# Two retention pieces per head freed from the gate buffer, one piece moved, and new planner constants, in a two-layer hybrid trunk

## The chip, the core and the metric

The kernel runs on one core of one Trainium2 chip (trn2). A core has five engines that run side by side, each through its own instructions in order: TensorE (PE, matrix multiplication and transposes), VectorE (DVE), ScalarE (ACT), GpSimd (POOL) and SyncE (SP, which here only issues DMAs). They meet through semaphores. The metric is the device time of one execution in microseconds; the number given for a kernel is the median of its runs.

## The reference

Two layers are computed over 1024 rows of width 1024. Each layer normalizes its input, multiplies it by one wide matrix (`w_in`), feeds the columns to three groups of heads, joins their outputs, multiplies by `w_out`, normalizes and adds to the input. Cut to what matters:

```
h = rmsnorm(x, pre_norm)
proj = einsum('bld,de->ble', h, w_in)
(gq, gk, gv, gz, gb, ga, sx, sB, sC, sz, sdt, rq, rk, rv, rg) = split_cols(proj, IN_SIZES)
qkv = silu(causal_conv(concat([gq, gk, gv]), gdn_conv))            # gated DeltaNet, 4 heads of 128
o_a = rmsnorm(gated_deltanet(...), gdn_norm) * silu(gz)
xbc = silu(causal_conv(concat([sx, sB, sC]), ssd_conv) + ssd_conv_b) # state space, 16 heads of 64, 2 groups
o_b = rmsnorm(ssd(...) * silu(sz), ssd_norm)
q_c, k_c = rotary(rq), rotary(rk)                                  # retention, 4 heads of 128
o_c = rmsnorm(retention(q_c, k_c, rv), ret_norm) * silu(rg)
x = x + rmsnorm(concat([o_a, o_b, o_c]) @ w_out, post_norm)
```

The DeltaNet solves, for each head and each chunk, a unit lower triangular system. Everything is float32; the kernel keeps that accuracy by splitting each factor of the large products into a high and a low part and summing three products.

## The kernel before

**Parts and pieces.** The work is cut into four parts, p = 0 to 3: two halves of 512 rows in each of two layers. Within a part, `w_in` is taken in 26 pieces of 256 columns, in the order of the list `PIECES` (L50): gate pieces of the DeltaNet ("gz"), its q, k, v ("gdn"), the B and C of the state space ("bc"), its gates ("sz", group, half) and inputs ("sx", group, half), and last eight retention pieces ("ret", 0) to ("ret", 7). The even retention pieces hold query and key of a head, the odd ones its value and gate. A piece has two halves, each with its own PSUM bank out of two, and a half is made in eight slices; a slice is 6 matmuls of 256 columns or 3 of 512.

**Weights.** Pieces go through a ring of two buffers (`W_RING`). A piece is loaded when the piece two before it has been used. ACT rounds it into the high part (L2147, four steps), and POOL subtracts to get the low part (L2433, four steps). Parts 0 and 2 do this for all pieces; they store the low parts in DRAM (the "keep" DMA, L1305), and parts 1 and 3 load them from there (L1302) beside the raw weights, so POOL has nothing to do. The pieces numbered in `AGAIN` (L63) are excepted: they are split again in parts 1 and 3 and not kept.

**Mixers.** Between the slices PE does the small products of the mixers. For the triangular systems a block of size `BASES[p]` (L39) on the diagonal is inverted on DVE column by column (`gdn_base`, L1844 to L1870), and then the inverse is doubled level by level on PE and DVE (`gdn_p`, `gdn_xx`; L1889, L1899, L1902) until it has 128 rows. `BASES` is (8, 16, 16, 16): part 0 has four levels, the others three. The finished rows of a group of heads stand in one of two gate buffers; `mix_turn` transposes them, and the units of the output projection (`out`, 24 matmuls each) use them.

**Gate buffers.** `gate_of` gives the gate buffer of a piece and `frees` (L877) lists the steps that must stand earlier in the order than a piece. A gate piece may come only after the `mix_turn` that read the buffer's earlier contents; so ("sz", 1, *) needs the `mix_turn` of DeltaNet heads (head 3 for the last piece), and every retention piece needs `mix_turn` of state-space group 0 (p, 1). A retention piece also needs its slot, which `x_turn` of the state space gives free.

**The order.** It is not made on the chip. `make_plan` (L242) keeps a clock for each engine with fixed costs, and puts out one list of steps; each engine runs its share of that list in that order. When several steps could be next, constants decide (L786 to L797). `OUT_WAIT` is the wait of the next mixer step above which an output unit is put in, provided that `APART` slices have passed since the last one; `LATE` says when a slice counts as late, so that an output unit goes first; `KEEP` and `HOLD` hold the last units of the second-last output group back.

Of the kernel before, what the change touches and what calls it, by code (L numbers as in the profile page):

```python
# [35 lines left out]
NDEC = GH + SH  # L36
NSM = GH + NDEC
LEVELS = 7
BASES = (8, 16, 16, 16)  # L39
FIRSTS = [n.bit_length() - 1 for n in BASES]  # L40
SIZES = sorted(set(BASES))
LOWEST, WIDEST = min(FIRSTS), max(BASES)
COPIES = 8
# [3 lines left out]

PC = 256
N_GDN_PC, N_GZ, N_BC, N_SZ, N_SX, N_RET = 6, 2, 2, 2, 2, 8
PIECES = ([("gz", 0), ("gdn", 0), ("gdn", 1), ("gz", 1), ("bc", 0), ("gdn", 2), ("gdn", 3), ("bc", 1),  # L50
           ("sz", 0, 0), ("gdn", 4), ("sz", 0, 1), ("gdn", 5), ("sz", 1, 0), ("sx", 0, 0), ("sx", 0, 1), ("sx", 1, 0),
           ("sx", 1, 1), ("sz", 1, 1)]
          + [("ret", i) for i in range(N_RET)])
AT = {piece: i for i, piece in enumerate(PIECES)}


def m_of(piece, half):

    return {"gdn": 0, "bc": 12}.get(piece[0], 16 + 4 * piece[1]) + 2 * piece[-1] + half


NTH = {m: n for n, m in enumerate(m_of(piece, half) for piece in PIECES if piece[0] in ("gdn", "bc", "sx") for half in range(2))}
AGAIN = range(3)  # L63
W_RING = 2
Q = KD
SBUF = 224 * 1024 - 1
# [65 lines left out]
def base_parts(size):  # L132

    out = [("mask", ()), ("sum", ())]
    for i in range(0, size, COPIES):
        out += [("copy", range(j, min(j + 4, i + COPIES))) for j in range(i, i + COPIES, 4)]
        out += [("column", range(j, min(j + 2, i + COPIES, size - 1))) for j in range(i, min(i + COPIES, size - 1), 2)]
    return out + [("spread", ()), ("turn", ())]


BASE_PARTS = [base_parts(n) for n in BASES]
BASE_END = [len(parts) - 1 for parts in BASE_PARTS]
# [50 lines left out]
def front_steps():  # L193
# [3 lines left out]
    def add(step, *needs):  # L197
        out.append((step, needs))
# [9 lines left out]
    for p in range(PARTS):  # L208
        for i, piece in enumerate(PIECES):
            for half in range(2):  # L210
                last = p + 1 < PARTS and (i, half) == (len(PIECES) - 1, 1)
                needs = list(frees(p, i, half))
                if i == 0 and p >= 2:
                    needs.append(("final", p - 2, NT - 1))
                if last:
                    for t in range(2):
                        add(("norm", p + 1, t), ("rescale", p + 1, t), *needs)
                if i == len(PIECES) - 2 and p + 1 < PARTS:
                    add(("scale", p + 1, half), ("ssd_y", p, SG - 1, NT - 1), *([("final", p - 1, NT - 1)] if p else []))
                for q in range(Q):  # L220
                    j, odd = divmod(Q * half + q - SPLIT_FROM, 2)
                    if 0 <= j < 4 and not odd and len(PIECES) * p + i + 1 < PARTS * len(PIECES):
                        add(("split", *((p, i + 1) if i + 1 < len(PIECES) else (p + 1, 0)), j))
# [18 lines left out]
def make_plan():  # L242
# [120 lines left out]
    def play(step):  # L363
# [9 lines left out]
        def mark(name, time):  # L373
            at[name] = time
# [99 lines left out]
        elif k == "gdn_base":  # L474
# [5 lines left out]
            elif part == "copy":  # L480
                mark("n", dve(len(cols) * (230 + 2 * BASES[p]), *after))
            elif part == "column":
                mark("n", dve(len(cols) * 2 * (220 + 2 * BASES[p]), *after))
            else:
# [231 lines left out]
    def due(step):  # L716
        return max([at.get(e, 0) for e in needs(step)] + [bank_due(step)])

    mix_at = inv_at = pre_at = front_at = apart = 0
    while mix_at < len(mix) or inv_at < len(inv) or pre_at < len(pre) or front_at < len(front) or outs or turns or any(sides.values()):  # L720
# [26 lines left out]
        if front_at < len(front) and front[front_at][0][0] == "split_small" and not ring_free():  # L747
            front_needs.append(("ring", ))
        wait = due(step) - now if step else OUT_WAIT + 1
        late = not front_needs and due(front[front_at][0]) > now + LATE  # L750
        stuck = any(n and n[0] not in ("split", "rescale") for n in front_needs) or front_at == len(front)
        unit = outs[0] if outs and ("small", smalls) in done and (outs[0][2] or not outs[0][1] or ("final", outs[0][1] - 1, NT - 1) in done) and (outs[0][1] % 2 or ("split_out", *outs[0][1:4]) in done) else None
        if unit and unit[1:3] == (PARTS - 1, GROUPS - 2):
            if front_at < len(front) and not stuck and len(outs) <= KEEP or front_at == len(front) and step and wait < HOLD:
                unit = None
        if unit and due(unit) <= now + NEAR and (late or stuck or wait > OUT_WAIT and apart >= APART):
            emit(outs.pop(0))
# [28 lines left out]
GATE_WAIT = 0  # L786
TABLE_WAIT = 1500
NORM_WAIT = 3000
OUT_WAIT = 1000000000.0
LATE = 200  # L790
SPLIT_FROM = 6
APART = 16
KEEP = 6
RELOAD = 4400
HOLD = 250
NEAR = 0
AHEAD = 2000  # L797
FAR = 1e12
# [16 lines left out]
def is_split(n):  # L815

    p, i = divmod(n, len(PIECES))
    return p % 2 == 0 or i in AGAIN


def is_kept(n):

    p, i = divmod(n, len(PIECES))
    return p % 2 == 0 and i not in AGAIN

# [45 lines left out]
def gate_of(p, i):  # L871

    kind = PIECES[i][0]
    return {"gz": 4 * p, "sz": 4 * p + 1 + (PIECES[i][1] if kind == "sz" else 0), "ret": 4 * p + 3}.get(kind)


def frees(p, i, half):  # L877
    need = []
    n = slot_of(p, i, half)
    if slot_owner(n) is not None:  # L880
        need.append(slot_reader(slot_owner(n)))
    g = gate_of(p, i)
    if g is not None and g >= 2:
        need.append(("mix_turn", p, 0, 2 * PIECES[i][2] + 1) if g % 4 == 2 else ("mix_turn", (g - 2) // 4, (g - 2) % 4))
    if PIECES[i] == ("sx", 0, N_SX - 1) and half == 1:
        need += [("gdn_p", p, GH - 2, LEVELS - 1, j) for j in range(2)]
    if PIECES[i] == ("sx", SG - 1, N_SX - 1) and half == 1:
        need += [("gdn_xx", p, GH - 1, LEVELS - 1, j) for j in range(2)]
    if PIECES[i][0] == "bc" and p:
        need.append(("ssd_y", p - 1, SG - 1, NT - 1))  # L890
    return need
# [52 lines left out]
def hybrid_kernel(nc, x, w_in, w_small, w_out, cons, rope, pars, rows, post_norm, out):  # L944
# [15 lines left out]
    with ExitStack() as ctx:  # L960
# [1129 lines left out]
        def _(act):  # L2090
# [20 lines left out]
            for s in plan:  # L2111
# [77 lines left out]
                elif k == "proj" and s[4] == Q - 1:  # L2189
# [33 lines left out]
                    elif kind in ("gz", "sz"):  # L2223
                        j = PIECES[i][-1]
                        G = gate_of(p, i)
                        gate_wait(act, G, p, PIECES[i])
                        empty(A(gate[:, G % 2, 2 * half:2 * half + 2, j * PC:(j + 1) * PC],
                                bank(tag).rearrange("p (t n) -> p t n", t=2), ACT.Silu), tag)
                    elif PIECES[i][1] % 2:
                        h = PIECES[i][1] // 2  # L2230
                        G = gate_of(p, i)
                        gate_wait(act, G, p, PIECES[i])
                        b = bank(tag).rearrange("p (t n) -> p t n", t=2)
                        v = slot_at(10 * p + 6 + h)[:, 1024:1536].rearrange("p (t n) -> p t n", t=NT)
                        slot_wait(act, 10 * p + 6 + h)
                        A(v[:, 2 * half:2 * half + 2, :], b[:, :, 0:P], ACT.Copy)
                        empty(A(gate[:, G % 2, 2 * half:2 * half + 2, h * P:(h + 1) * P], b[:, :, P:2 * P], ACT.Silu), tag)
# [248 lines left out]
```

How the kernel before makes its waits and increments, by code:

```python
        def wait_filled(eng, tag):  # L1097
            eng.wait_ge(filled[bank_of[tag]], use_of[tag] + 1)
# [1 line left out]
        def wait_emptied(eng, tag):  # L1100
            eng.wait_ge(emptied[bank_of[tag]], use_of[tag] + 1)
# [94 lines left out]
        def slot_wait(eng, n):  # L1196
            if slot_owner(n) is None:
                return
            r = slot_reader(slot_owner(n))
            if r[0] == "gdn_open":
                wait_filled(eng, (*r, "a"))
                eng.wait_ge(S["gdn_kq"], GH * r[1] + r[2] + 1)
            elif r[0] == "x_turn":
                wait_filled(eng, (*r, NT - 1))
            else:
                wait_filled(eng, r)
# [22 lines left out]
        @block.sync  # L1230
# [3 lines left out]
                if kind == "later":  # L1234
                    sp.dma_start(con[:, C_LEV:], cons[:, C_LEV:]).then_inc(later, 16)
                    for l in range(1, DEPTH):
                        sp.dma_start(par[:, l, :], pars[l]).then_inc(later, 16)
                elif kind == "x":
                    if n >= NT:
                        wait_filled(sp, ("norm", (n - 2) // NT, (n - 2) % NT, 1))
                    if p and key[2] < 2:
                        wait_filled(sp, ("ssd_y", p - 1, SG - 1, NT - 1, "w"))
                    if p >= 2:
                        sp.wait_ge(x_stored[key[2]], 16 * (p - 1))
                    sp.dma_start(x_tile(n), x_rows(p, key[2])).then_inc(x_in[n if n < 4 else n % 2], 16)
                elif kind == "rest" and p == PARTS - 1:
                    wait_filled(sp, ("ret_o", p, RH - 1, NT - 1))
```

## Time and profile before

| | |
|---|---|
| median of 3 runs | 2102.42 us (2098.83 to 2102.58) |
| the profiled execution, its own time | 2098.74 us |
| its span, from the first to the last instruction | 2096.9 us |
| PE busy | 2042.2 us |
| DVE busy | 1414.8 us |
| ACT busy | 995.7 us |
| POOL busy | 516.1 us |

The span is what the instructions of the core take; the execution's own time is 1.8 us more. An engine's busy time counts matmuls that overlap in the pipeline once. Parts are not marked in the profile. By the order of the matmuls, the slices of part 0 run from 14 to 494 us, of part 1 to 1001 us, of part 2 to 1529 us and of part 3 to 2028 us; after that come the last output units, to 2085 us. The granted clock of TensorE is given as a share of full speed: 1.0 is 2.4 GHz and 0.5 is 1.2 GHz.

### The profile page before, as it was taken

The page shows a single profiled execution, that of the slowest core. Times are in us where ns is not written, and L with a number is a line of the kernel's source. Part 1 is how long each engine was busy: PE and PEld are TensorE (multiplying, and loading weights), DVE is VectorE, ACT ScalarE, POOL GpSimd, SP SyncE. Part 2 cuts the span into 40 slices and gives each one's busy share as a digit, 9 for nine tenths or more (in the row PEclk, how much of TensorE's full clock was granted, in tenths as well). Part 3 has the DMA queues.
Part 4 walks back from the last instruction along what each step waited for, and adds up shares of the span by engine and source line. Part 5 has one row for each costly group of instructions (what it writes and reads, how often), then busy time and mean ns, then how long its engine had stood idle before and what let it go on. Part 6 is the DMA issues. An engine that isn't in the chain of part 4 may idle for free.

```text
span 2096.9 us, 38540 instructions
## 1 busy us (share of the span) xinstructions
PE 2042.2 (97%) x14692; PEld 1885.2 (90%) x14692; DVE 1414.8 (67%) x3324; ACT 995.7 (47%) x1985; POOL 516.1 (25%) x456
## 2 busy tenths in 40 slices
PE   7999999999999999999999999899999999999997
PEld 6888888999989988999889897899989899899997
DVE  5788767546668877734578888675566788766334
ACT  5644376434554447633454344664345444574211
POOL 3443343432101102201243334334320011121001
PEclk9999999999999999999999999999999999999999
DMA  4543255545555635344354436455546546453434
GB/s 167 169 141 99 106 185 174 191 153 191 196 176 181 212 131 208 134 160 135 120 189 141 141 113 210 161 182 171 190 131 233 180 162 212 150 181 121 161 108 185
DMA packets 88119, 343.57 MB, mean 164 GB/s; under 512 B 10048, under 2 KB 11136, under 8 KB 81536
## 3 DMA queue, kind: packets, MB, share of 16 engines
q1 hardware_dynamic: 87360, 340.69, 47.8%
q8 instruction: 118, 1.93, 0.4%
q14 instruction: 65, 0.53, 0.1%
q10 hardware_dynamic: 576, 0.41, 0.1%
HBM read 250.72 MB, written 90.34 MB: 163 GB/s over the span
## 4 chain that ended last, share of the span: by engine, by line
PE 87%; DVE 5%; issue 4%; ACT 3%; POOL 1%; DMA 0%; POOLq 0%; DVEq 0%; SPq 0%; ACTq 0%
PE ps L1367 83%; PE ps L1370 4%; POOL w_low L2433 1%; ACT wk L2306 0%; ACT w_hi L2147 0%; POOL rs L2390 0%; ACT L2242 0%; DVE base L1862 0%; DVE wo_parts L1990 0%; DVE base L1863 0%; DMA wk<-in_x 0%; DVE wk L1934 0%; DVE slot L1759 0%; ACT raw L2207 0%; ACT slot L2242 0%
## 5 line engine op out<-in xcount | busy, mean ns | idle before, releaser
L1367 PE MATMUL ps<-w_hi,hT_hi 128*128 128x256 f32 x1792 | 524.5, 293 | 4.7 <-POOL w_low L2433 3.0
L1367 PE MATMUL ps<-w_hi,hT_lo 128*128 128x256 f32 x1792 | 504.0, 281 | 0.0
L1367 PE MATMUL ps<-w_low,hT_hi 128*128 128x256 f32 x1792 | 502.7, 281 | 0.0
L2433 POOL TENSOR_TENSOR w_low<-w_loaded,w_hi 128x512 fp32r<-128x512 f32 x232 | 314.1, 1372 | 470.9 <-ACT w_hi L2147 470.7
L1367 PEld LDWEIGHTS ps<-w_hi,hT_hi 128*128 128x128 f32 x1792 | 340.3, 190 | 11.8 <-POOL w_low L2433 4.3
L1367 PEld LDWEIGHTS ps<-w_low,hT_hi 128*128 128x128 f32 x1792 | 338.1, 189 | 5.0 <-issue 4.3
L1367 PEld LDWEIGHTS ps<-w_hi,hT_lo 128*128 128x128 f32 x1792 | 338.2, 189 | 0.0
L1367 PE MATMUL ps<-hT_hi,w_hi 128*128 128x512 f32 x768 | 319.0, 415 | 5.2 <-POOL w_low L2433 5.2
L1367 PE MATMUL ps<-hT_hi,w_low 128*128 128x512 f32 x768 | 304.0, 396 | 0.0
L1367 PE MATMUL ps<-hT_lo,w_hi 128*128 128x512 f32 x768 | 303.6, 395 | 0.0
L1367 PE MATMUL ps<-wo_parts,mixT_hi 128*128 128x256 f32 x960 | 269.9, 281 | 0.0
L1759 DVE SCALAR_TENSOR_TENSOR slot<-raw,par,slot 128x512 f32<-128x512 f32 x222 | 190.6, 859 | 17.3 <-ACT slot L2220 11.5
L2004 DVE TENSOR_TENSOR acc<-acc,ps 128x512 f32<-128x512 f32 x96 | 65.6, 686 | 184.4 <-PE ps L1367 177.4
L1367 PEld LDWEIGHTS ps<-wo_parts,mixT_hi 128*128 128x128 f32 x960 | 180.9, 188 | 3.3 <-issue 2.4
L1367 PEld LDWEIGHTS ps<-hT_hi,w_hi 128*128 128x128 f32 x768 | 145.5, 189 | 32.8 <-POOL w_low L2433 7.0
L1367 PEld LDWEIGHTS ps<-hT_lo,w_hi 128*128 128x128 f32 x768 | 144.6, 188 | 32.7
L1367 PEld LDWEIGHTS ps<-hT_hi,w_low 128*128 128x128 f32 x768 | 145.4, 189 | 24.9 <-issue 0.2
L2147 ACT ACTIVATE w_hi<-w_loaded 128x512 fp32r<-128x512 f32 x232 | 135.2, 623 | 64.6 <-DMA w_loaded<-in_w_in 64.5
L1367 PE MATMUL ps<-wk 128*128 128x128 f32 (+2 forms) x1008 | 156.5, 287 | 2.4 <-issue 1.3
L1367 PEld LDWEIGHTS ps<-wk 128*128 128x128 f32 x1008 | 135.0, 192 | 21.3 <-issue 10.4
L2147 ACT ACTIVATE w_hi<-w_raw 128x512 fp32r<-128x512 f32 x184 | 107.8, 622 | 81.3 <-DMA w_low<-w_low_kept 81.2
L1367 PE MATMUL ps<-wo_hi,mixT_hi 128*128 128x256 f32 x480 | 139.6, 291 | 4.3 <-DVE wk L2008 2.9
(225 smaller groups left out, 3969.3 us busy)
## 6 DMA issues: line engine op xcount, KB each, us to landing
w_loaded<-in_w_in SPq DMA_DIRECT2D x116, 512.0 KB, 5.1
w_low_kept<-w_low SPq DMA_DIRECT2D x46, 1024.0 KB, 8.1
w_raw<-in_w_in SPq DMA_DIRECT2D x92, 512.0 KB, 5.8
w_low<-w_low_kept SPq DMA_DIRECT2D x92, 512.0 KB, 6.7
wo_loaded<-in_w_out SPq DMA_DIRECT2D x32, 512.0 KB, 4.1
wk<-cum_rows SPq DMA_DIRECT2D x32, 512.0 KB, 3.8
wo_split<-wo_parts SPq DMA_DIRECT2D x32, 512.0 KB, 7.7
wo_parts<-wo_split SPq DMA_DIRECT2D x28, 512.0 KB, 4.4
```

Of the source, the lines that this page charges most:

```text
L1367: return nc.tensor.matmul(o, a, b, start=start, stop=stop)
L1370: return nc.tensor.transpose(o, a, ident)
L1759: stt(o, r[:, j:j + HALF], w[:, j:j + 1], o, ALU.mult, ALU.add).then_inc(S["conv_done"], 1)
L2004: empty(tt(o, o, b, ALU.add), s)
L2147: A(high, source, ACT.Copy).then_inc(S["w_hi_ready"], 1)
L2433: tt(w_lo[at], wr[at], w_hi[at], ALU.subtract)\
```

## The change

Six things differ, and everything else follows from the list of steps that the planner makes of them:

- `gate_of` gives no gate buffer for even retention pieces (query and key). They have no gate columns, and `frees` therefore no longer asks for `mix_turn` (p, 1) before them.
- ("ret", 0) stands ahead of ("sz", 1, 1) in `PIECES`. Among the DeltaNet and B/C pieces the order becomes gdn 2, bc 0, bc 1, gdn 3 (it was bc 0, gdn 2, gdn 3, bc 1).
- `BASES[2]` is 8, so part 2 inverts blocks of 8 and doubles over four levels, as part 0 does.
- `AGAIN` is pieces 1 and 2; piece 0, ("gz", 0), is kept in DRAM by parts 0 and 2 and loaded by parts 1 and 3.
- `OUT_WAIT` is 1000, `LATE` 0, `KEEP` 2 and `HOLD` 0.
- The plan follows from all these.

```
-BASES = (8, 16, 16, 16)
+BASES = (8, 16, 8, 16)
...
-PIECES = ([("gz", 0), ("gdn", 0), ("gdn", 1), ("gz", 1), ("bc", 0), ("gdn", 2), ("gdn", 3), ("bc", 1),
+PIECES = ([("gz", 0), ("gdn", 0), ("gdn", 1), ("gz", 1), ("gdn", 2), ("bc", 0), ("bc", 1), ("gdn", 3),
            ("sz", 0, 0), ("gdn", 4), ("sz", 0, 1), ("gdn", 5), ("sz", 1, 0), ("sx", 0, 0), ("sx", 0, 1), ("sx", 1, 0),
-           ("sx", 1, 1), ("sz", 1, 1)]
-          + [("ret", i) for i in range(N_RET)])
+           ("sx", 1, 1), ("ret", 0), ("sz", 1, 1), ("ret", 1), ("ret", 2), ("ret", 3), ("ret", 4), ("ret", 5),
+           ("ret", 6), ("ret", 7)])
...
-AGAIN = range(3)
+AGAIN = range(1, 3)
...
-OUT_WAIT = 1000000000.0
-LATE = 200
+OUT_WAIT = 1000
+LATE = 0
...
-KEEP = 6
+KEEP = 2
...
-HOLD = 250
+HOLD = 0
...
-    return {"gz": 4 * p, "sz": 4 * p + 1 + (PIECES[i][1] if kind == "sz" else 0), "ret": 4 * p + 3}.get(kind)
+    return {"gz": 4 * p, "sz": 4 * p + 1 + (PIECES[i][1] if kind == "sz" else 0), "ret": 4 * p + 3 if PIECES[i][1] % 2 else None}.get(kind)
```

## Rows read from the trace of the kernel before

**Rows 1.** Page: busy time, share of the span, number of instructions; TensorE.

```profile
PE 2042.2 (97%) x14692; PEld 1885.2 (90%) x14692; DVE 1414.8 (67%) x3324; ACT 995.7 (47%) x1985; POOL 516.1 (25%) x456
```

**Rows 2.** Windows: stretch, length, busy us of each engine (instructions), clock, DMA.

```profile
600.00:800.00 200.00, 200.00 (x1323) 180.85 (x1322) 155.80 (x465) 99.17 (x192) 20.50 (x24) 1.00 0.52 174
1200.00:1300.00 100.00, 95.14 (x621) 85.57 (x620) 84.95 (x206) 43.25 (x90) 40.40 (x34) 0.98 0.46 156
1300.00:1345.00 45.00, 39.02 (x249) 34.23 (x247) 31.52 (x47) 26.69 (x60) 16.79 (x13) 0.92 0.38 129
```

**Rows 3.** Waits of PE, 1100 to 1345 us: total us, times, longest.

```profile
PE ps L1370 <- DVE gate L1955: 5.5, 1, 5.5
PE ps L1367 <- POOL w_low L2433: 4.3, 2, 3.1
PE ps L1367 <- DVE st_g L1927: 1.9, 1, 1.9
```

**Rows 4.** Waits of PE, 300 to 345 us.

```profile
PE ps L1367 <- DVE wk L1692: 1.5, 1, 1.5
PE ps L1367 <- DVE wk L2008: 1.4, 1, 1.4
```

**Rows 5.** Windows at half clock, columns as in rows 2.

```profile
323.60:327.00 3.40, 3.40 (x12) 2.37 (x11) 3.40 (x7) 0.00 (x0) 0.00 (x0) 0.50 0.68 231
1197.40:1200.80 3.40, 3.40 (x11) 2.69 (x9) 2.08 (x19) 0.76 (x2) 0.29 (x1) 0.50 0.94 337
1289.60:1293.00 3.40, 3.40 (x14) 3.12 (x13) 3.33 (x6) 0.78 (x2) 1.29 (x1) 0.50 0.40 166
1323.70:1330.50 6.80, 3.47 (x16) 3.47 (x17) 4.22 (x5) 6.77 (x18) 4.18 (x4) 0.50 0.06 22
```

**Rows 6.** Timeline of PE, 1310 to 1330 us: start, us, instruction, idle before it.

```profile
1319.65 1.91 PE L1370 MATMUL ps<-con,slot 128*128 128x128 f32 x16
1327.03 1.11 PE L1370 MATMUL ps<-con,gate 128*128 128x128 f32 x4 [5.47 <-DVE gate L1955]
```

**Rows 7.** Chain that ended last, 895 us on: start, us, matmuls.

```profile
895.74 31.86 PE ps L1367 x272
```

**Rows 8.** Windows, DVE with tile base, in parts 0, 1 and 2.

```profile
60.00:280.00 220.00, 32.93 (x132) 0.99 0.40 133
500.00:820.00 320.00, 41.08 (x260) 1.00 0.52 173
1000.00:1310.00 310.00, 58.13 (x260) 0.99 0.45 151
```

**Rows 9.** Lines by form, DVE, 60 to 280 us: count, busy us, mean ns.

```profile
L1902 DVE TENSOR_TENSOR slot<-ps,con 128x256 f32<-128x256 f32 x32 | 12.6, 402 | 2.6 <-PE ps L1367 2.5
L1889 DVE TENSOR_TENSOR wk<-wk,ps 128x256 f32<-128x256 f32 x24 | 9.5, 414 | 2.2 <-PE ps L1367 1.8 <-DVE wk L1908 0.2
L1899 DVE STREAM_TRANSPOSE wk<-wk 128x256 f32<-128x256 f32 x16 | 6.9, 431 | 0.0
```

**Rows 10.** Timeline of PE, 110 to 131 us: the products of one step, then a slice.

```profile
123.44 1.05 PE L1367 MATMUL ps<-slot,wk 128*128 128x128 f32 x8
124.25 0.48 PE L1367 MATMUL ps<-hT_hi,w_hi 128*128 128x512 f32 x1
```

**Rows 11.** DMA issues: count, KB each, median us to landing.

```profile
w_loaded<-in_w_in SPq DMA_DIRECT2D x116, 512.0 KB, 5.1
w_low_kept<-w_low SPq DMA_DIRECT2D x46, 1024.0 KB, 8.1
w_low<-w_low_kept SPq DMA_DIRECT2D x92, 512.0 KB, 6.7
```

**Rows 12.** Timeline of SP's queue, 0 to 110 us: the load of piece 2.

```profile
29.47 0.81 SPq L1299 DMA_DIRECT2D w_loaded<-in_w_in  x2
```

**Rows 13.** Waits of all engines, whole span, columns as in rows 3.

```profile
DVE et L2036 <- POOL et L2411: 19.7, 4, 7.3
```

**Rows 14.** Lines by form, DVE, 345 to 495 us: emptying a retention piece's bank.

```profile
L1784 DVE TENSOR_TENSOR slot<-ps,rp 128x256 f32<-128x256 f32 x16 | 6.7, 417 | 3.9 <-PE ps L1367 3.3 <-DVE gate L1969 0.6
```

## The prediction

> **What bounds the kernel now.** I read the engines' busy times first. PE is busy for 2042.2 us of the span, and no other engine reaches 70% [rows 1]. The reader should see that little can be won: a kernel bound by one engine can lose only that engine's idle time, its time at half clock, or work. So I looked for these stretch by stretch. In the DeltaNet stretch of part 1 PE is never idle in 200 us, although DVE is busy for 78% of it [rows 2]. Part 2 is different. In the 100 us from 1200 us on PE is idle for 4.9 us with DVE at 85%, and in the 45 us after that for 6.0 us with the clock at 0.92 [rows 2]. The waits of PE name the reasons: one of 5.5 us for the last step of a DeltaNet head (L1955), two of 4.3 us in all for low weights, and 1.9 us behind DVE [rows 3]. A second, smaller place is the first state-space group of part 0 [rows 4]. Four stretches at half clock lie beside these places: 3.4 us at 323.6, 1197.4 and 1289.6 us, and 6.8 us at 1323.7 us [rows 5]. Waits of the other engines count only where PE shows them.
>
> **The retention piece as filler.** In part 2 PE ends the 16 transposes of `x_turn` at 1321.6 us and stands until 1327.0 us, for `mix_turn` of head 3 [rows 6]. The order had nothing else to give it: ("sz", 1, 1) needs that very `mix_turn`, part 1's output units were used up, and the retention pieces stood behind. After the change ("ret", 0) needs only `x_turn` and stands next. 272 narrow matmuls take 31.86 us, 117 ns each, so a half of 48 takes 5.6 us and the piece 11.2 us [rows 7]. That is more than the wait of 5.5 us. The wait goes, and the half clock at 1323.7 us with it: for 3.3 of its 6.8 us PE stood anyway; in the other 3.5 us it worked at half rate and lost 3.5 / 2 = 1.75 us [rows 5, 6]. Gain: 5.5 + 1.75 = 7.2 us. The lower end is nothing, if the planner still puts `mix_turn` straight behind `x_turn`.
> In part 0 the same piece can stand among the steps of state-space group 0, where PE waits 1.5 + 1.4 us and then works 3.4 us at half clock, a loss of 1.7 us [rows 4, 5]. Together that is 4.6 us. These waits stand at single steps behind DVE's masks, and a filler helps only where the order puts it into the right gap. Between 0 and 4.6 us I take two thirds, 3.0 us, since the order is made from clocks that know of masks. What is moved is no new work: the loads follow the use of the ring, and the matmuls are the same. Parts 1 and 3 still have output units as filler in this stretch, so they gain nothing.
>
> **Blocks of 8 in part 2.** Removed on DVE: the base steps cost 58.1 us in part 2, and with blocks of 8 in part 0, also beside POOL's subtractions, 32.9 us; 25.2 us less [rows 8]. Added on DVE: one level for 4 heads, each with two masks (402 ns), two subtractions (414 ns) and two transposes (431 ns): 4 x 2 x 1.247 = 10.0 us [rows 9]. DVE is relieved by 15.2 us. Added on PE: 4 heads x 2 halves x (4 + 4) = 64 matmul instructions. Eight of them take 0.81 us from their start to that of the next slice, so 64 take 6.5 us [rows 10].
> The Trainium skill (TensorE: Matmul & The Clock Gate, section Back-to-back issue gap) gives about 81 ns per matmul of 128 columns in a stream with its weight loads. As an estimate the 64 would cost 5.2 us by it; the row has 101 ns for each, and the measurement decides.
> What DVE's relief gives to PE is bounded by what PE loses there beside the 5.5 us: 1.9 us behind DVE and 4.3 us behind the split of weights [rows 3], and two half clocks of 3.4 us, 1.7 us each [rows 5]: 9.6 us. The lower end is 0. The wait behind DVE and the half clocks should go (1.9 + 3.4 us). Of the 4.3 us I take 3.5: POOL's subtraction is slow beside DVE's many small steps, but it also hangs on the load before it. That is 8.8 us; net of the matmuls, 8.8 - 6.5 = 2.3 us gained.
> The same 260 base steps take 58.1 us in part 2 and 41.1 us in part 1, where POOL hardly subtracts [rows 8]. The Trainium skill (SBUF — State Buffer, section Who interferes with whom) says that a DVE step with two SBUF inputs and a GpSimd step hold a shared port in turn, and the loser waits for the whole instruction. By that rule the added steps, which read PSUM or one SBUF input, keep their price whatever POOL does. It would leave the 10.0 us as they are.
>
> **Piece 0 kept.** Parts 1 and 3 save four subtractions and load 1 MB more; parts 0 and 2 store 1 MB more. In parts 1 and 3 a load is issued two pieces ahead, so it has one piece of 11.2 us before its first slice [rows 7], and one of these lands in 6.7 us [rows 11]. In part 0 the store stands on SP's queue ahead of the load of piece 2, which needs its buffer: today that load is issued at 29.5 us [rows 12]. The store can begin when the four low parts are made, about 28 us by the order of POOL's steps, lands after 8.1 us, and the load after another 5.1 us [rows 11], at 41 us; ACT and POOL then need 2 us, and piece 2 starts at 45 us. This is close. I take 0, with 3 us of loss and 1 us of gain as bounds. Behind the store on SP's queue stand the loads of piece 2 and of the next output unit, which ACT splits; no mixer step waits for them yet.
>
> **Order of the DeltaNet pieces and the constants.** Head 1 gets its keys one piece (11 us) earlier, head 2 one piece later; head 2 opens only after head 1 in both orders. `OUT_WAIT` and `LATE` let output units in sooner, so that fewer are left later, above all at the end of part 3, where nine stand behind its last slice. Bounds: 4 us either way, a bit less than two such waits as the longest here [rows 3]; 0 taken. For waits at new places in a new order I add 2.0 us, one wait like the 1.9 us of today [rows 3].
>
> **Sum.** -7.2 - 3.0 - 2.3 + 2.0 = -10.5 us. Against the profiled execution, 2098.7 us, that gives 2088.2 us. The median of the runs before stands 3.7 us above that execution, so the forecast for a median is 2091.9, say 2092 us.
>
> **Rivals.** (a) *All of it works.* The 4.6 us of part 0 and the 9.6 us of part 2 go in full, and no new wait comes: -7.2 - 4.6 - 9.6 + 6.5 = -14.9 us, 2087.5 us; with the constants' 4 us it ends at 2083.5, and with what I can't see in rows somewhat below. For it: the part 1 stretch shows PE without idle time beside a DVE nearly as busy [rows 2].
> (b) *The wait moves.* The planner's clock thinks head 3 done earlier than it is and puts its `mix_turn` ahead of the retention piece or after a slice or two of it. Then the 7.2 us stay, and 3.0 + 2.3 - 2.0 = 3.3 us are left: 2099 us; with the lower ends of the other terms more than 2102. For it: the order before was made by the same clock and was wrong by 5.5 us there [rows 3]. Against: DVE, whose lateness makes it wrong, is relieved by 15.2 us. That the change doesn't do what it says (the piece comes no earlier, since its slot needs `x_turn` anyway) gives the same time.
> (c) *The retention piece stalls its own bank: slower.* The piece in this place, ("sz", 1, 1), is emptied by ACT in one step. ("ret", 0) is emptied by DVE, in order, in four steps of 0.42 us [rows 14], and DVE stands in waits of its own in the state-space stretch: up to 7.3 us for POOL (L2036) [rows 13]. A bank has 5.6 us of cover, the other half [rows 7]. With 1.7 us for emptying, the deciding point is a DVE wait of 3.9 us. The longest row would cost 7.3 + 1.7 - 5.6 = 3.4 us. If four of the eight halves met such a wait, 13.6 us, and two of these brought a half clock of 1.7 us, it would be -10.5 + 17.0 = +6.5 us, 2109 us. Against: the four such waits sum to 19.7 us, a mean of 4.9 us, just over the point [rows 13].
>
> **Chances.** Forecast (2087 to 2097) 0.48; (a), below that, 0.17; (b) 0.20, of which 0.04 below 2098.2; (c) 0.15. About 0.2%, 4.2 us, is what a measurement of this kernel can tell from no change. Faster 0.48 + 0.17 + 0.04 = 0.69; same 0.16 of (b) and 0.01 of (c), 0.17; slower 0.14. The range leaves out the outer half of (c) and the far end of (a): 2080 to 2109 us.
>
> **What would show it.** In the changed kernel's trace the wait for L1955 behind `x_turn` of part 2 is gone, and matmuls of a narrow piece stand there; the half clock at about 1324 us is gone; DVE's base steps in part 2 take about 33 us in 132 instructions; PE has 14692 + 64 matmuls; its idle time between 1200 and 1345 us falls from 10.9 us to under 4. If PE waits for DVE's L1786, which empties the bank, (c) is at work; if it waits for L2147 or L2433 near 45 us or at the start of part 1 or 3, the kept piece is. Wrong at the root would be a large gain or loss in parts 1 and 3 or at the end: then the constants decide, which I put at 0.

## The result, and the profile after

The changed kernel takes 2105.75 us (median; 2101.69 to 2108.64), the kernel before 2101.08 us beside it (2098.83 to 2103.48). The ratio is 1.0021, 95% interval 1.0013 to 1.0030: it is slower by about 4.7 us, where I had forecast 2092 us. The profiled span is 2102.9 us, 6.0 us longer than before. (The title counts wrongly: of the two retention pieces of each head one is freed, the one with query and key.)

The page of the changed kernel, and windows of part 2 (stretch, length, busy us of PE, PEld, DVE, ACT, POOL with instructions, clock, DMA). They answer to [rows 1] and [rows 2]:

```profile
PE 2052.4 (98%) x14756; PEld 1894.6 (90%) x14756; DVE 1417.3 (67%) x3220; ACT 1002.9 (48%) x1991; POOL 514.8 (24%) x448
...
1200.00:1300.00 100.00, 98.13 (x650) 87.74 (x649) 73.36 (x150) 41.05 (x88) 39.60 (x36) 1.00 0.54 186
1300.00:1345.00 45.00, 43.16 (x296) 37.92 (x295) 31.05 (x55) 29.31 (x61) 19.16 (x14) 1.00 0.41 141
```

DVE alone with tile base, in the stretch of part 2, answers to the last of [rows 8]:

```profile
1000.00:1310.00 310.00, 32.80 (x132) 1.00 0.47 157
```

In part 2 the signs that I had named came true. Idle time of PE between 1200 and 1345 us fell from 10.9 to 3.7 us, the clock of that stretch is 1.00, the base steps take 32.8 us. The waits of PE from 1100 to 1345 us (total, times, longest) no longer hold the 5.5 us for L1955, and those for L2433 fell from 4.3 to 1.3 us [rows 3]:

```profile
PE ps L1367 <- POOL w_low L2433: 1.3, 3, 0.8
PE ps L1367 <- DVE slot L1902: 0.9, 3, 0.5
```

So the time was lost elsewhere. The waits of PE over the whole span show two groups that before did not have at all, L2147 and the DMA of `wo_parts`:

```profile
PE ps L1370 <- ACT wk L2123: 9.1, 1, 9.1
PE ps L1367 <- POOL w_low L2433: 8.8, 9, 2.5
PE ps L1367 <- ACT w_hi L2147: 4.2, 2, 2.2
PE ps L1367 <- DMA wo_parts<-wo_split: 2.9, 1, 2.9
```

The 9.1 us are in both kernels. The half clock stretches have moved: in place of those at 323.6, 1197.4, 1289.6 and 1323.7 us [rows 5] there are these (besides one near 61 us and one behind the last matmuls, which both kernels have):

```profile
294.90:301.70 6.80, 6.10 (x27) 5.81 (x28) 3.59 (x3) 6.74 (x13) 2.29 (x2) 0.50 0.45 186
516.70:520.10 3.40, 3.40 (x18) 3.40 (x18) 0.69 (x1) 3.40 (x5) 0.74 (x2) 0.50 0.16 58
2059.60:2063.00 3.40, 3.40 (x18) 3.40 (x17) 0.00 (x0) 0.00 (x0) 0.00 (x0) 0.51 1.03 417
```

**An account of the whole span.** A window that is 5 us worse says little when the order of steps differs. So I gave each matmul its step of the planned order, took the time from the start of each step to that of the next, and took as usual length of a kind of step the 15th percentile of the kernel before. What a step has above it is a stall where it is 0.25 us or more, and small excess where it is less. This holds both waits and half clock. It is my own working from the starts of the matmuls, in us:

| kernel | first to last matmul | usual work | small excess | stalls | part 0 | part 1 | part 2 | part 3 | end |
|---|---|---|---|---|---|---|---|---|---|
| before | 2072.8 | 1942.5 | 64.9 | 65.4 | 22.0 | 5.6 | 28.4 | 5.6 | 0.5 |
| after | 2078.8 | 1948.4 | 68.2 | 62.2 | 25.4 | 9.2 | 11.2 | 7.9 | 5.2 |

(Another 3.3 us of stalls lie before the first slice, in all kernels. The account is of one execution. A second profiled execution of experiments 1, 2 and 3 differs in single columns by up to 2 us, so smaller differences between kernels say nothing.) Part 2 has 17.2 us less of stalls. Against it stand 5.9 us of matmuls of the added level, 3.3 us of small excess, and stalls: 3.4 us in part 0, 3.6 us in part 1, 2.3 us in part 3, 4.7 us at the end. The sum is +6.0 us.

### The profile page after: what moved, and what is told of

Read it like the earlier page. It is cut to its first block, busy times and chain, and to the rows that moved or that the text cites. A ratio compares the mean times of both kernels' runs of the same rounds, so it can differ in the third digit from the quotient of the medians.

```text
span 2102.9 us, 38565 instructions
## 1 busy us (share of the span) xinstructions
PE 2052.4 (98%) x14756; PEld 1894.6 (90%) x14756; DVE 1417.3 (67%) x3220; ACT 1002.9 (48%) x1991; POOL 514.8 (24%) x448
## 4 chain that ended last, share of the span: by engine, by line
PE 82%; DVE 5%; issue 4%; DMA 4%; ACT 3%; POOL 1%; SPq 1%; POOLq 0%; DVEq 0%; ACTq 0%
PE ps L1367 79%; PE ps L1370 4%; DMA wo_split<-wo_parts 1%; DMA w_low_kept<-w_low 1%; DMA wk<-in_x 1%; DVE slot L1759 1%; POOL w_low L2433 1%; ACT wk L2306 0%; DMA wk<-x_mid 0%; ACT w_hi L2147 0%; DVE hT_lo L1711 0%; ACT L2242 0%; DVE acc L2082 0%; ACT wk L2297 0%; DVE wo_parts L1990 0%
## 5 line engine op out<-in xcount | busy, mean ns | idle before, releaser
L2433 POOL TENSOR_TENSOR w_low<-w_loaded,w_hi 128x512 fp32r<-128x512 f32 x224 | 310.4, 1403 | 436.8 <-ACT w_hi L2147 436.8
L2147 ACT ACTIVATE w_hi<-w_raw 128x512 fp32r<-128x512 f32 x192 | 112.2, 623 | 104.7 <-DMA w_low<-w_low_kept 104.7
L1367 PEld LDWEIGHTS ps<-wk 128*128 128x128 f32 x1024 | 135.6, 191 | 21.0 <-issue 11.5
L2147 ACT ACTIVATE w_hi<-w_loaded 128x512 fp32r<-128x512 f32 x224 | 129.7, 621 | 39.4 <-DMA w_loaded<-in_w_in 39.4
```

The source lines that it names most:

```text
L1367: return nc.tensor.matmul(o, a, b, start=start, stop=stop)
L2147: A(high, source, ACT.Copy).then_inc(S["w_hi_ready"], 1)
L2433: tt(w_lo[at], wr[at], w_hi[at], ALU.subtract)\
```

## The experiments

All ratios are to the kernel before on the same chip, with the 95% interval; one part in a thousand is 2.1 us. A difference of two ratios is uncertain by 1.2 to 2.0 in a thousand, by their intervals. The stalls named in this section are from the account above.

**1. The retention part alone**, in the kernel before.

```
-           ("sx", 1, 1), ("sz", 1, 1)]
-          + [("ret", i) for i in range(N_RET)])
+           ("sx", 1, 1), ("ret", 0), ("sz", 1, 1)]
+          + [("ret", i) for i in range(1, N_RET)])
...
-    return {..., "ret": 4 * p + 3}.get(kind)
+    return {..., "ret": 4 * p + 3 if PIECES[i][1] % 2 else None}.get(kind)
```

> The kernel before with the gate freed for even retention pieces and (ret, 0) ahead of (sz, 1, 1), and nothing else; the planner makes the order again. Theory A (this part of the change is worth what was forecast, and the loss comes from other parts): PE's 5.5 us wait for L1955 in part 2 and the half clock beside it go, 7 us; part 0 gives back 3 us, since the weights of (ret, 0) come late there; 2097 us against 2101 before, ratio 0.998. Theory B (the freed piece only moves the waits, here too): 2101 us or more, ratio 1.000 or above.

Measured: 1.0044 [1.0030, 1.0058], 9 us slower. The wait for L1955 in part 2 is gone, and stalls there fell from 28.4 to 22.3 us; but part 0 has 31.4 in place of 22.0 us, and the end 3.8 in place of 0.5. The waits of PE from 340 to 372 us are new:

```profile
PE ps L1367 <- ACT wk L2297: 4.0, 1, 4.0
PE ps L1370 <- ACT gate L2324: 4.0, 1, 4.0
```

L2324 makes the gated rows that `mix_turn` (0, 1) transposes, and ("ret", 1) still needs that `mix_turn`, since odd pieces keep their gate columns. The piece that used to stand between had been used 11 us earlier, and few output units were left as cover. The wait had moved by one piece: from `mix_turn` of head 3 to `mix_turn` of state-space group 0.

**2. Blocks of 8 in part 2 alone**, in the kernel before.

```
-BASES = (8, 16, 16, 16)
+BASES = (8, 16, 8, 16)
```

> The kernel before with blocks of 8 in part 2 and nothing else. Theory A (the level pays for itself): the 64 added matmul instructions cost 6 us, the waits behind DVE and the half clocks between 1100 and 1303 us give 8 us; 2099 us, ratio 0.999. Theory B (DVE's relief is not what PE lacked, the matmuls are simply added): 2106 us, ratio 1.002 to 1.003; then this alone would be the whole loss of the changed kernel.

Measured: 1.0003 [0.9995, 1.0012]. PE is busy for 2048.7 us, 6.5 us more; DVE for 1400.8 us, 14.0 us less; part 2 has 21.4 us of stalls in place of 28.4 (20.7 us in a second execution). The matmuls of the added level take what the relief of DVE gives. In this order PE still waits for L1955, by the same 5.5 us:

```profile
PE ps L1370 <- DVE gate L1955: 5.5, 1, 5.5
```

**3. Piece 0 split again**, in the changed kernel.

```
-AGAIN = range(1, 3)
+AGAIN = range(3)
```

> The changed kernel with piece 0 split again in parts 1 and 3, as before (AGAIN = range(3)); the rest of the order stays almost the same. Theory A (the kept piece costs the two waits for L2147 at the third slice of part 1 and of part 3): both waits of 2.2 us and the half clock near 517 us go; 2100 us against 2105.7 for the changed kernel, ratio to before 0.9995. Theory B (the waits there come from the later output units and the order, not from the load): the waits stay, 2105 us, ratio 1.002.

Measured: 0.9993 [0.9985, 1.0002]. The loss is gone: 2.8 in a thousand less than the changed kernel, 5.9 us. Stalls of part 1 and 3 are 5.4 and 6.0 us, as before. But it isn't the 10 us gain that I forecast either.

**4. The old `OUT_WAIT`** in the changed kernel.

```
-OUT_WAIT = 1000
+OUT_WAIT = 1000000000.0
```

> The changed kernel with OUT_WAIT at 1e9 again, the rest as changed. Theory A (the earlier output units cost the end of part 3, where PE waits 2.9 us for the weights of a unit and then runs at half clock, and 3 us of switching between slices and units): 2099 us, ratio to before 0.999. Theory B (the constant is neutral, the loss at the end comes from somewhere else): 2105 us, ratio 1.002.

Measured: 1.0048 [1.0034, 1.0062]. The constant is worth 2.7 in a thousand, 5.7 us, in the new order. (Both theories expected it to cost or to do nothing.) Putting back `KEEP` and `HOLD` leaves the list of steps as it is, word for word; they do nothing here.

**5 and 6. The order apart from the data path.** The planner reads `AGAIN` too, so experiment 3 also changed the order. Here the plan is made with one value and the kernel built with the other.

```
+    global AGAIN
+    own, AGAIN = AGAIN, PLAN_AGAIN
     plan = make_plan()
+    AGAIN = own
```

Experiment 5 has `AGAIN = range(3)` and `PLAN_AGAIN = range(1, 3)`: the changed kernel's order, with piece 0 split again. Experiment 6 has them the other way round: the order of experiment 3, with piece 0 kept.

> The changed kernel's order of steps to the last one (its planner still believes that piece 0 is kept), but piece 0 is in fact split again in parts 1 and 3 and not stored. Theory A (the data path: 1 MB more to load and to store delays the loads of x, behind which ACT's fourth split of piece 0 stands): the waits of PE at the third and fourth slice of parts 1 and 3 go, ratio to before 0.9993 as with AGAIN = range(3), 2099 us. Theory B (the planner's order, with the split of an output unit put later, makes those waits): ratio 1.002, 2105 us, with the waits in place.

> The mirror image: the order of the kernel with AGAIN = range(3), but piece 0 is kept and loaded. Theory A (data path): PE waits for L2147 come back at the start of parts 1 and 3, ratio 1.002, 2104 us. Theory B (order): none, ratio 0.9993, 2099 us. Together with the run before this splits the 6 us between the two; if both land midway, both matter.

Measured: experiment 5 0.9992 [0.9983, 1.0000], experiment 6 1.0001 [0.9992, 1.0009]. The order of the changed kernel alone is not at fault. Keeping the piece costs 2.9 in a thousand in it (6.1 us); in the order of experiment 3 it costs 0.8 (1.7 us), which is within the uncertainty. How the loss comes about is seen at the start of part 1. First the longest wait of SP's queue from 489 to 505 us, then SP, ACT and PE from 488 to 516 us, all of the changed kernel (start, us, instruction, idle before it):

```profile
SPq L1331 <- DMA wo_split<-wo_parts: 10.4, 1, 10.4
```

```profile
488.38 0.33 SPq L1301 DMA_DIRECT2D w_raw<-in_w_in  x1
488.75 0.43 SPq L1302 DMA_DIRECT2D w_low<-w_low_kept  x1
...
491.01 0.53 SPq L1310 DMA_DIRECT2D wo_split<-wo_parts  x1
501.96 0.33 SPq L1335 DMA_DIRECT2D wo_loaded<-in_w_out  x1
...
503.28 1.41 SPq L1305 DMA_DIRECT2D w_low_kept<-w_low  x1
504.73 2.61 SPq L1245 DMA_DIRECT2D wk<-in_x  x2
```

```profile
513.33 1.06 ACT L2119 ACTIVATE junk<-wk 128x1024 f32<-128x1024 f32 x1 [5.21 <-DMA wk<-in_x]
...
514.38 0.61 ACT L2147 ACTIVATE w_hi<-w_raw 128x512 fp32r<-128x512 f32 x1
```

```profile
515.04 0.38 PE L1367 MATMUL ps<-w_hi,hT_hi 128*128 128x256 f32 x1 [2.19 <-ACT w_hi L2147]
```

Read it from the end, that is from the wait of PE. PE waits 2.19 us for the fourth rounding step of ("gz", 0). ACT takes its steps in order, and that one stands behind the norm of the next rows of x (L2119), which waits 5.21 us for its load. The weights had landed, since three of the four steps were done. The load of x is issued at 504.73 us without a wait of its own, straight behind what stands ahead of it on SP's queue, and that queue had stood 10.4 us, until 501.96, for the store of an output unit's low part (L1310, 491.01) to land. That store was issued right behind the kept piece's loads, which bring 1 MB more. In experiment 5, with the same order and no kept piece, SP and ACT have these lines (its line numbers are four higher):

```profile
SPq L1335 <- DMA wo_split<-wo_parts: 7.1, 1, 7.1
```

```profile
502.96 1.57 SPq L1249 DMA_DIRECT2D wk<-in_x  x2
...
509.13 1.06 ACT L2123 ACTIVATE junk<-wk 128x1024 f32<-128x1024 f32 x1 [3.74 <-DMA wk<-in_x]
...
510.18 0.62 ACT L2151 ACTIVATE w_hi<-w_loaded 128x512 fp32r<-128x512 f32 x1
```

The same store lands 3.3 us sooner after its issue, the load of x lands 6.2 us after its issue in place of 8.6, ACT's fourth step begins 4.2 us earlier, and PE does not wait. In the changed kernel the half clock at 516.7 us follows the wait. Part 3 begins with the same wait, of 2.0 us.

In experiment 6 the piece is kept too, and ACT's fourth step is nearly as late, at 513.4 us. But its order has 24 matmuls of an output unit (from 512.92 us) and `ret_s` between the third slice and the fourth, which begins only here:

```profile
516.56 0.37 PE L1371 MATMUL ps<-w_hi,hT_hi 128*128 128x256 f32 x1
```

In the changed kernel the same 24 matmuls stand behind the fourth slice. So at this place the loss needs two things together: the kept piece makes the load of x late, and the order made for it has moved the filler away.

**7. Keeping the piece alone**, in the kernel before.

```
-AGAIN = range(3)
+AGAIN = range(1, 3)
```

> The kernel before with one edit: piece 0 is kept in DRAM and loaded in parts 1 and 3 instead of split again; order and constants stay those of before. Theory A (keeping costs by itself, because its loads and stores crowd SP's queue at the starts of parts, whatever the order): slower by about 6 us, ratio 1.002 to 1.004, with PE waits for L2147 at the starts of parts 1 and 3. Theory B (keeping costs only together with the order of the changed kernel, in which the loads of part 0's output units and of x stand late): no wait for L2147 there, ratio 0.999 to 1.001.

Measured: 1.0032 [1.0019, 1.0045], 6.7 us slower. The size is that of theory A, but the wait isn't where either theory had it: PE never waits for L2147. Lines of SP, ACT and PE from 480 to 499 us, for piece 0 kept:

```profile
480.52 1.21 SPq L1245 DMA_DIRECT2D wk<-in_x  x2
...
488.75 1.06 ACT L2119 ACTIVATE junk<-wk 128x1024 f32<-128x1024 f32 x1 [5.53 <-DMA wk<-in_x]
...
492.95 0.59 ACT L2330 ACTIVATE wk<-ps 128x512 f32<-128x512 f32 x1
...
493.60 0.65 PE L1370 MATMUL ps<-con,gate 128*128 128x128 f32 x4 [1.56 <-ACT wk L2330]
...
498.96 0.68 PE L1367 MATMUL ps<-slot,wk 128*128 128x128 f32 x4 [1.69 <-issue]
```

and of the kernel before:

```profile
478.20 1.20 SPq L1245 DMA_DIRECT2D wk<-in_x  x2
...
485.00 1.06 ACT L2119 ACTIVATE junk<-wk 128x1024 f32<-128x1024 f32 x1 [5.36 <-DMA wk<-in_x]
...
488.67 0.60 ACT L2330 ACTIVATE wk<-ps 128x512 f32<-128x512 f32 x1
```

x is issued 2.3 us later, because the planner, which takes the kept piece into its clocks, puts an output unit ahead of PE's step that frees the buffer; and it lands 8.2 us after its issue in place of 6.8. So it arrives 3.75 us later, and L2330, behind L2119 on ACT, is 4.3 us late. Here the step that PE misses is not the split of the piece but L2330, a step of retention's last head. This comes twice, before part 1 and before part 3, with 1.6 + 1.7 and 1.4 + 1.7 us of waits, 6.4 us. The profiled execution is 9.2 us longer than that of the kernel before; much of the rest is in part 2, where the half clock near 1290 us is 6.8 us long in place of 3.4. (For the 1.7 us the profile names no releaser; that they come from the same delay is inferred.)

**8. The old order of the DeltaNet and B/C pieces**, with piece 0 split again.

```
-AGAIN = range(1, 3)
+AGAIN = range(3)
...
-PIECES = ([("gz", 0), ("gdn", 0), ("gdn", 1), ("gz", 1), ("gdn", 2), ("bc", 0), ("bc", 1), ("gdn", 3),
+PIECES = ([("gz", 0), ("gdn", 0), ("gdn", 1), ("gz", 1), ("bc", 0), ("gdn", 2), ("gdn", 3), ("bc", 1),
```

> The changed kernel with piece 0 split again, and the DeltaNet and B/C pieces in their old order (bc 0, gdn 2, gdn 3, bc 1). It is to be read against the same kernel with the new order (0.9993 of before). Theory A (the order of these pieces is worth nothing, as forecast): 0.998 to 1.001. Theory B (it is part of why stalls in part 2 fell): above 1.002, with the lost time in part 2 before 1320 us.

Measured: 1.0038 [1.0025, 1.0050] against 0.9993 with the new order. The order that I priced at nothing is worth 4.5 in a thousand, 9.4 us. Theory B has the size, but not the place: part 2 has 10.7 us of stalls with the old order and 12.4 with the new. The time is lost in part 0 (26.6 against 24.8), part 1 (9.2 against 5.4), part 3 (11.5 against 6.0) and at the end (5.4 against 3.3). In part 0 PE waits, from 340 to 372 us:

```profile
PE ps L1370 <- ACT gate L2324: 5.5, 1, 5.5
```

In the new order head 3 ends later: its `mix_turn` stands at 300 us, not at 285 us. The output units that need it start at 308 us in place of 295 us, and four of them stand between `x_turn` (0, 1) and `mix_turn` (0, 1), not two. At 2.8 us each they cover the 5.5 us. So the later head keeps the fillers back for the place where they are needed. The other parts, 1 and 3, were not followed to single waits.

**9. The retention part with the new `OUT_WAIT`**, in the kernel before: experiment 1 and

```
-OUT_WAIT = 1000000000.0
+OUT_WAIT = 1000
```

> The kernel before with the retention part (even pieces need no gate buffer, ret 0 ahead of sz 1 1) and OUT_WAIT 1000; LATE, KEEP, HOLD, bases, piece order and piece 0 as before. The retention part alone was 1.0044 of before. Theory A (the loss came from output units used up early, so that nothing covered the wait for ret 1's gate in part 0; OUT_WAIT changes when they are used): the 8 ms-style stall at 349 to 369 us of part 0 shrinks from about 12 us to under 4 us and the ratio is 0.998 to 1.001. Theory B (the loss is the retention part's own, whatever the constant): ratio 1.003 to 1.006.

Measured: 1.0064 [1.0050, 1.0078]. Both theories miss, B by little. I had thought that the constant was the partner that makes the retention part pay. It isn't: stalls of 3.8 + 5.8 + 1.3 us stand again around `mix_turn` (0, 1), and with the old piece order the constant costs 2.0 in a thousand, as much as the uncertainty of this difference, where it earns 2.7 with the new.

**10. The changed kernel without the retention part**, with piece 0 split again: the edit of experiment 1 undone.

> The changed kernel with AGAIN = range(3) and with the retention part of the change taken back: the gate buffer is waited for by all eight pieces, and (ret, 0) stands behind (sz, 1, 1). Theory A (freeing the retention pieces only moves the waits, as in the first experiment, where it cost 9 us alone): the wait for L1955 in part 2 is back, but part 0 and the end give as much or more; ratio 0.997 to 0.999, at or below AGAIN = range(3). Theory B (with output units let in early, OUT_WAIT = 1000, the freed piece is worth its 5 us and more): ratio 1.001 to 1.003.

Measured: 1.0029 [1.0018, 1.0040] against 0.9993 with it. In the new order the retention part earns 3.6 in a thousand, 7.6 us. Without it the waits of PE from 1300 to 1400 us are

```profile
PE ps L1370 <- DVE gate L1955: 5.5, 1, 5.5
PE ps L1370 <- ACT gate L2324: 2.7, 1, 2.7
```

so the wait of [rows 6] is back with its old length, with blocks of 8 too. Two more things stand in its account (in the table of the next section). Part 0 has 23.4 us of stalls, against 24.8 with the retention part and 22.0 in the kernel before: PE waits 2.8 us for L1955 where the changed kernel waits for its weights. And the end has 0.5 us of stalls in place of 3.3, with no wait for `wo_parts`. That wait is there in every kernel with the retention part and the old place of the loads of x, from 2.6 to 3.9 us, and in none without the part.

**11. The last loads of x behind those of the tail**, with piece 0 split again. At the end of part 3 the changed kernel issues four loads of x between the loads of the output units. The key by which a load is put into SP's queue is raised:

```
-            loads.append((where["ret_o", p, RH - 1, NT - 1] if p == PARTS - 1 else
+            loads.append((max(where["ret_o", p, RH - 1, NT - 1], where["out", PARTS - 1, GROUPS - 2, UNITS - 3, NT // 2 - 1]) + 0.5 if p == PARTS - 1 else
```

> The changed kernel with AGAIN = range(3), and at the end of part 3 the four loads of x for the last step stand on SP's queue behind the loads of the last output units, not ahead of them. Theory A (these 2 MB stand ahead of the load for unit (3, 2, 3), for which PE waits 2.6 us and then works at half clock): the wait for wo_parts at about 2050 us goes, 3 to 4 us less than with AGAIN = range(3) alone, ratio 0.998, 2095 us. Theory B (that load is late because it is issued late, by the order of the units, and its neighbours on the queue do not matter): no change, ratio 0.9993.

Measured: 0.9978 [0.9969, 0.9987], 2095.51 us: faster than both kernels, the one before and the changed one. SP's queue in the changed kernel, and then in this one (one load of each left out, and some of the tail's eight loads):

```profile
2047.21 1.75 SPq L1248 DMA_DIRECT2D wk<-x_mid  x4
...
2050.45 0.39 SPq L1338 DMA_DIRECT2D wo_parts<-wo_split  x1
```

```profile
2045.29 0.97 SPq L1338 DMA_DIRECT2D wo_parts<-wo_split  x1
...
2051.34 1.91 SPq L1248 DMA_DIRECT2D wk<-x_mid  x4
```

In the kernel before, the loads of x stood behind the units' loads as well:

```profile
2048.52 0.38 SPq L1338 DMA_DIRECT2D wo_parts<-wo_split  x1
...
2053.59 1.99 SPq L1248 DMA_DIRECT2D wk<-x_mid  x4
```

Their place in the queue goes by the step `ret_o` of the last head. With the retention part this step comes just ahead of the output step whose end frees the buffer for the last unit's weights, and in the kernel before just behind it. The waits of PE from 2020 us on fall from 2.9 us in the changed kernel to

```profile
PE ps L1367 <- DMA wo_parts<-wo_split: 0.8, 1, 0.8
```

and the half clock at 2059.6 us is gone. Against experiment 3 it is 1.5 in a thousand, 3.1 us.

**12. Experiment 11 with blocks of 16 in part 2.**

> The changed kernel with piece 0 split again, the last x loads behind the tail's loads, and blocks of 16 in part 2 again. It is to be read against the same kernel with blocks of 8 (0.9978 of before). Theory A (blocks of 8 return what their 64 matmuls cost and no more): 5.9 us of matmuls less and as much more stall in part 2, ratio 0.997 to 0.999. Theory B (they pay, since DVE sets the end of the DeltaNet stretch in the new order too): ratio 0.999 to 1.003, with waits for DVE above 10 us in part 2. Theory C (they only cost): 0.995 to 0.997.

Measured: 0.9997 [0.9988, 1.0006] against 0.9978. Blocks of 8 pay 1.9 in a thousand, 4.0 us, in this order, where they paid nothing in the old one. Part 2 has 23.0 us of stalls in place of 12.2, so 10.8 us less for 5.9 us of matmuls. The waits of PE from 1240 to 1345 us without blocks of 8:

```profile
PE ps L1367 <- POOL w_low L2433: 5.0, 5, 2.9
PE ps L1367 <- DVE wk L1870: 3.7, 1, 3.7
```

L1870 is the last of the base steps: DVE is late with the block itself. The mechanism is theory B's (though the waits for DVE are 3.7 us, not 10, and 5.0 us stand for POOL), and the ratio lies in its range.

## Why the prediction was wrong

The step that failed is the one on the piece that is kept: "I take 0, with 3 us of loss and 1 us of gain as bounds". It costs 6.1 us, by a late load of x that ACT waits for (experiments 5 and 7). Without it (experiment 3) the change still gives 0.9993 in place of 0.995: the retention piece gains nothing in part 0 (forecast -3.0 us), and it costs about 3 us at the end, a term that the forecast put at nothing. And the order and the constants, taken as 0, decide what the other parts give; the order of the pieces alone is worth 9.4 us. That 2105.75 us lies within the outer range of 2080 to 2109 us is luck: rival (c) set its upper end, and (c) did not occur.

The accounts of the kernels that decide, in us, with columns as above:

| kernel | first to last matmul | usual work | small excess | stalls | part 0 | part 1 | part 2 | part 3 | end |
|---|---|---|---|---|---|---|---|---|---|
| 1, retention alone | 2083.1 | 1942.5 | 65.4 | 75.2 | 31.4 | 7.4 | 22.3 | 6.8 | 3.8 |
| 1, second execution | 2080.9 | 1942.5 | 65.2 | 73.2 | 30.1 | 7.7 | 20.9 | 6.3 | 4.9 |
| 3, piece 0 split again | 2071.5 | 1948.4 | 67.9 | 55.2 | 24.8 | 5.4 | 12.4 | 6.0 | 3.3 |
| 3, second execution | 2070.2 | 1948.4 | 68.3 | 53.5 | 23.0 | 5.4 | 11.9 | 6.0 | 3.8 |
| 7, kept alone | 2082.1 | 1942.5 | 64.7 | 74.8 | 23.3 | 7.5 | 32.8 | 7.5 | 0.5 |
| 8, old piece order | 2081.7 | 1948.4 | 66.6 | 66.7 | 26.6 | 9.2 | 10.7 | 11.5 | 5.4 |
| 10, without retention | 2082.5 | 1948.4 | 67.4 | 66.8 | 23.4 | 6.1 | 23.2 | 10.3 | 0.5 |
| 11, late x | 2069.9 | 1948.4 | 68.1 | 53.5 | 24.8 | 5.4 | 12.2 | 6.3 | 1.5 |
| 12, late x, blocks of 16 | 2073.8 | 1942.5 | 67.6 | 63.7 | 26.2 | 5.4 | 23.0 | 5.3 | 0.5 |

**Retention piece as filler in part 2 (-7.2 us): right.** The wait went, and comes back with the same 5.5 us without the part (experiment 10). I had forecast -7.2 - 8.8 = -16.0 us of stalls in part 2 for both parts together; they are -16.0 us in experiment 3 and -17.2 us in the changed kernel. Taken singly in the old order the parts give less there, -6.1 us (experiment 1) and -7.0 us (experiment 2). In the new order each is worth more, 10.8 us (experiments 10 against 3, and 12 against 11). So the mechanism is right, but that the sum came out to the number is partly luck.

**The same piece in part 0 (-3.0 us): it gained nothing.** Part 0 has 2.8 us more of stalls than before in experiment 3 (1.0 us in its second execution), and 3.4 us more in the changed kernel. Not all of this is the piece's: without it (experiment 10) part 0 has 1.4 us more as well. The waits of [rows 4] are gone, but ("ret", 0) comes to PE before its own weights are split. The waits of PE from 285 to 305 us, and ACT's steps before them, in the changed kernel:

```profile
PE ps L1367 <- POOL w_low L2433: 3.1, 2, 2.5
```

```profile
287.76 0.66 ACT L2147 ACTIVATE w_hi<-w_loaded 128x512 fp32r<-128x512 f32 x1
288.28 2.45 ACT L2306 ACTIVATE wk<-wk,cum 128x128 f32<-128x128 f32 x8
290.75 1.28 ACT L2308 ACT_TABLE_LOAD   x1
292.05 1.06 ACT L2308 ACTIVATE wk<-wk 128x1024 f32<-128x1024 f32 x1
293.01 1.14 ACT L2147 ACTIVATE w_hi<-w_loaded 128x512 fp32r<-128x512 f32 x2
```

The last two of four rounding steps stand 4.8 us behind steps of the state space, POOL's subtraction follows them, and beside the wait 6.8 us at half clock begin. I wrote that "what is moved is no new work". That is true and says nothing on where ACT has the split.

**Blocks of 8 (-2.3 us): right in the mechanism; its worth hangs on the order.** DVE's base steps take 32.8 us against 32.9 forecast, DVE is relieved by 14.0 us (experiment 2) against 15.2, and the relief is worth 7.0 to 10.8 us against 8.8. The 64 matmuls cost 5.9 us in the account and 6.5 us of PE's busy time, against 6.5 us from [rows 10]; the estimate of 5.2 us by the Trainium skill (TensorE: Matmul & The Clock Gate, section Back-to-back issue gap) is too low here. The net is 0 in the old order and -4.0 us in the new. In the changed kernel DVE's whole busy time did not fall (1417.3 against 1414.8 us): part 0 alone has 13.7 us more of it, with no step added there. A mean step of L1968 went from 802 to 962 ns and of L1692 from 1246 to 1324 ns. Other neighbours on POOL may be the reason; no run tests it.

**Piece 0 kept (0, at most 3 us of loss): the step that turned the sign.** It costs 6.1 us in the changed order (the changed kernel against experiment 5) and 6.7 us alone (experiment 7), twice my bound. I looked for the cost at ("gdn", 1), where the store stands ahead of a load in part 0, and at the kept piece's own landing. Both were no trouble. It costs where it makes the next load of x late, by 1 MB more in the queues ahead of it or by the order that the planner makes with it, because ACT waits for x in order and holds the steps behind it: the split of the piece, or a step of retention. In the trace of before ACT already waited 5.4 us for that load, with no wait of PE behind it. The prediction read the waits of PE only, and wrote that waits of other engines count only where PE shows them; they also show which slack a later load would use up. And my sentence on the queue stopped at part 0's first pieces: at the seams between parts I did not list what stands behind the new DMAs.

**The order of the pieces and the constants (0, bounds 4 us): mis-sized.** The bound does not follow from its row: two waits as long as the longest of [rows 3] are 11.0 us, and 4 us is less than one. The piece order is worth 9.4 us (experiment 8 against 3), `OUT_WAIT` 5.7 us (experiment 4). Neither number is a property of the edit. The retention part loses 9.2 us with the old piece order and gains 7.6 us with the new; `OUT_WAIT` gains 5.7 us with the new and loses 4.2 us, just at the limit of what can be told, with the old. I summed the parts as if each gave in any order what it gives in its own, and that sum is the second mistake. What I had named as the sign of being wrong at the root, a loss in parts 1 and 3 and at the end, is what the account shows.

**The end (0): 3 us lost, by the retention part.** The forecast has no row for the loads behind the last slice, and says of the moved piece that "the loads follow the use of the ring". The four loads of x don't: they came ahead of the last unit's weights in SP's queue, and only in kernels with the retention part (experiment 10 has no such loss). Experiment 11 gets most of the time back.

**New waits (+2.0 us).** The small excess alone grew by 3.3 us; 1.7 us of it are in experiment 2 with the added level. The rest was not explained; it is not a greater number of changes between kinds of steps, which are 1109 in the changed kernel and 1111 before.

Put together for experiment 3, which is the change without the kept piece: forecast -10.5 us, the account -1.3 us. Of the 9.2 us between, 5.8 are in part 0 (-3.0 forecast, +2.8 found) and 2.8 at the end; the rest is in small terms. The second execution of experiment 3 gives -2.6 us, with 1.8 us less in part 0, so this split holds to about 2 us. The kept piece adds the other 6 us.

**Rivals.** (b), the wait moves, is out for part 2, but in part 0 its relative is seen in experiments 1, 8 and 9: the wait moves to `mix_turn` (0, 1). (c) is out: PE has no wait for L1786 or L2036 in any of the kernels, and L2036's wait for POOL fell from 19.7 [rows 13] to 5.9 us in the changed kernel. The loss came by a road that no rival held, though the list of signs named the start of parts 1 and 3 for the kept piece, and it was seen there.

**What stays open.** The cost of keeping piece 0 in the order of experiment 3, 1.7 us, is not told from none. Why the piece order and `OUT_WAIT` pay in parts 1 and 3 was not followed wait by wait. `LATE` was not tried apart.

## What to carry to other kernels

Where a kernel runs on a planned order, a load that is added costs whatever stands behind it on its queue and then behind the first engine that waits for it: list that at every seam of the program, and look for waits of other engines that are still covered, since they mark the places without slack. Fillers are a stock: a piece used earlier to cover one wait is missing at the next, so look for the next step that needs a filler before you count the gain. Effects of ordering changes don't add up; where a change comes as a bundle found by a search, single prices hold only beside the others, and the range must be wider than the sum of them.

## What the runs showed of the hardware

Short waits can bring more than their own length. In the changed kernel a wait of 2.2 us that ends at 515.0 us is followed by a stretch of 3.4 us at 1.2 GHz from 516.7 us on, and the 2.9 us that end at 2058.6 us by 3.4 us from 2059.6 us on; beside the wait of 2.5 us that ends at 295.0 us there are 6.8 us at that clock. But it is not certain: the wait of 2.0 us at the start of part 3 has none behind it, nor have the waits of 1.6 and 1.7 us in experiment 7, nor the wait of 3.2 us that ends at 2051.5 us in the second execution of experiment 3. A stretch of 3.4 us of matmuls at half rate costs 1.7 us, and one of 6.8 us up to 3.4 us. So I would now price a wait of 2 to 3 us in such a stream of matmuls with nothing to 3.4 us more, and mostly 1.7.
